# Two transformer blocks in one kernel: the first block's second half runs on 256 columns instead of 272, and its loops are written out

## The reference

```python
h = concatenate([meta, x], axis=1)                       # 16 + 256 tokens of 1024
u = rmsnorm(h, norm_mix_w); proj = u @ w_in
y_pool = pool_mixer(...)                                 # trailing windows of 2, 4, 8, 16 tokens
y_gla  = gla_mixer(...)                                  # gated linear attention, in chunks of 64
h = h + concatenate([y_pool, y_gla], -1) @ w_out         # token by token from here on
h = h + hier_moe(rmsnorm(h, norm_ffn_w), ...)            # 1 of 4 groups, 2 of its 4 experts
return rmsnorm(h, final_norm_w)[:, N_META:]              # the meta tokens' rows are dropped

def hier_moe(x, ...):
    combine = ...                                        # (tokens, 16) shares of the experts
    for e in range(16):
        y += combine[:, e] * ((silu(x @ w_gate[e]) * (x @ w_up[e])) @ w_down[e])
```

## Time and profile before

| | |
|---|---|
| Median of three runs | 2490.15 us |
| The profiled execution | 2492.44 us |
| Its span, first to last instruction | 2490.7 us |
| TensorE busy | 2289.7 us, 92% |
| VectorE busy | 1400.7 us, 56% |
| ScalarE busy | 779.3 us, 31% |
| GpSimd busy | 541.8 us, 22% |
| Mean granted TensorE clock | 0.953 |
| DMA over the span | 314.70 MB, 126 GB/s |

### The profile page before, as it was taken

How to read it: one execution, slowest core, us unless ns; L and a number is a source line. 1 busy time by engine, 2 the same in 40 slices (tenths; PEclk the granted TensorE clock), 3 DMA queues, 4 the chain that set the end, 5 groups by cost and what they waited for, 6 DMA issues and landing times.

```text
span 2490.7 us, 32942 instructions
## 1 busy us (share of the span) xinstructions
PE 2289.7 (92%) x12803; PEld 1938.0 (78%) x12803; DVE 1400.7 (56%) x1714; ACT 779.3 (31%) x1065; POOL 541.8 (22%) x298
## 2 busy tenths in 40 slices
PE   6686999979999998978989999989999997888997
PEld 5675999967888886855768888868888776658997
DVE  5635555766555547755477775555564225554444
ACT  3323444333222213244232222123222223344443
POOL 1001344003222002147132221013222001172430
PEclk9767999989999998989999999989999998999999
DMA  5302666853453454510245554444453334303663
GB/s 165 126 17 57 179 171 186 245 161 110 132 146 111 138 154 133 144 51 1 85 135 169 168 170 131 144 129 133 129 147 98 93 93 116 107 1 102 186 169 118
DMA packets 473572, 314.70 MB, mean 126 GB/s; under 512 B 26976, under 2 KB 435431, under 8 KB 473463
## 3 DMA queue, kind: packets, MB, share of 16 engines
q1 hardware_dynamic: 434294, 237.69, 34.2%
q10 hardware_dynamic: 39168, 75.51, 9.5%
HBM read 312.10 MB, written 1.05 MB: 126 GB/s over the span
## 4 chain that ended last, share of the span: by engine, by line
PE 78%; DVE 8%; ACT 5%; POOL 4%; issue 3%; DMA 1%; SPq 1%; POOLq 0%; DVEq 0%; ACTq 0%
PE ps L1394 23%; PE ps L1396 23%; PE ps L1395 23%; PE ps L1454 3%; POOL s L1376 2%; DVE ada_acc L866 2%; PE ps L1411 2%; ACT w_hi L555 2%; PE ps L1387 1%; POOL u_lo L1325 1%; DVE rstd L880 1%; DVE u_hi L894 1%; DVE st L1252 1%; ACT tmp_b L616 1%; PE ps L1741 1%
## 5 line engine op out<-in xcount | busy, mean ns | idle before, releaser
L1394 PE MATMUL ps<-u_hi,w_hi 128*128 128x512 f32 (+2 forms) x2528 | 883.0, 349 | 70.2 <-POOL u_lo L1325 59.8
L1395 PE MATMUL ps<-u_lo,w_hi 128*128 128x512 f32 (+2 forms) x2528 | 871.7, 345 | 0.0
L1396 PE MATMUL ps<-u_hi,w_lo 128*128 128x512 f32 (+2 forms) x2528 | 871.3, 345 | 0.0
L842 DVE TENSOR_TENSOR w_lo<-raw,w_hi 128x2048 fp32r<-128x2048 f32 (+1 forms) x238 | 504.7, 2121 | 235.4 <-ACT w_hi L555 234.5
L555 ACT CAST w_hi<-raw 128x2048 fp32r<-128x2048 f32 (+1 forms) x238 | 418.3, 1758 | 638.3 <-PE ps L1396 590.3
L1394 PEld LDWEIGHTS ps<-u_hi,w_hi 128*128 128x128 f32 x2528 | 485.2, 192 | 141.4 <-issue 65.4
L1396 PEld LDWEIGHTS ps<-u_hi,w_lo 128*128 128x128 f32 x2528 | 485.0, 192 | 54.2
L1395 PEld LDWEIGHTS ps<-u_lo,w_hi 128*128 128x128 f32 x2528 | 485.5, 192 | 52.1 <-issue 0.5
L866 DVE SCALAR_TENSOR_TENSOR ada_acc<-ada_w,sc_c,ada_acc 128x512 f32<-128x512 f32 x504 | 385.1, 826 | 4.4 <-DMA ada_w<-in_w_ada 4.4
L1332 POOL TENSOR_TENSOR hf_lo<-tmp_b,hf_hi 128x512 f32 (+3 forms) x88 | 230.9, 2624 | 644.2 <-ACT hf_hi L639 644.2
L635 ACT ACTIVATE tmp_a<-ps 128x512 f32<-128x512 f32 (+2 forms) x120 | 60.6, 505 | 729.4 <-PE ps L1396 650.3
(11 more groups left out here) (241 smaller groups left out, 1917.3 us busy)
## 6 DMA issues: line engine op xcount, KB each, us to landing
ada_w<-in_w_ada ACTq DMA_DIRECT2D x144, 512.0 KB, 3.6
raw<-in_w_ffn_gate SPq DMA_DIRECT2D x88, 512.0 KB, 4.0
raw<-in_w_ffn_up SPq DMA_DIRECT2D x88, 512.0 KB, 5.3
raw<-in_w_in SPq DMA_DIRECT2D x52, 512.0 KB, 4.7
raw<-in_w_ffn_down SPq DMA_DIRECT2D x64, 384.0 KB, 3.3
raw<-in_w_ffn_down SPq DMA_DIRECT2D x64, 320.0 KB, 3.8
raw<-in_w_expert_gate SPq DMA_DIRECT2D x32, 512.0 KB, 4.2
raw<-in_w_expert_up SPq DMA_DIRECT2D x32, 512.0 KB, 5.4
```

Source lines behind the costliest of these rows:

```text
L842: tt(w_lo[:, slot, 0:elems], raw[:, slot, 0:elems], w_hi[:, slot, 0:elems].bitcast(F32), ALU.subtract).then_inc(lo_done.sem, 1)
L1394: mm(acc, w1, m_hi, start=(first and i == 0), stop=False)
L1395: mm(acc, w1, m_lo, start=False, stop=False)
L1396: ins = mm(acc, w2, m_hi, start=False, stop=(last and i == n - 1))
```

## The change

Everything of the first block behind the mixer that ran on columns 0 to 271 runs on the 256 columns from 16 on: the output projection (its moving operand starts at column 16 of `u_hi` and `u_lo`), the residual's addition, the norm, the router, the experts. `h1` keeps its 272 columns, the new results go to columns 16 to 271. The router has two groups of 128 tokens instead of three. The mixers, which need the meta tokens, stay as they are.

`repeat` no longer makes a loop: all bodies of all ten stages, the second block's too, are written out on every engine.

```diff
 def repeat(eng, n, body):
-    if n <= 3:
-        for i in range(n):
-            body(i)
-        return
-    body(0)
-    with eng.Fori(1, n - 1) as i:
+    for i in range(n):
         body(i)
-    body(n - 1)
...
-        R2 = carve([("hm_hi", [P, MOE_F, T1], F32R), ("hm_lo", [P, MOE_F, T1], F32R), ("comb", [P, N_EXPERTS, T1], F32)])
+        R2 = carve([("hm_hi", [P, MOE_F, SEQ], F32R), ("hm_lo", [P, MOE_F, SEQ], F32R), ("comb", [P, N_EXPERTS, SEQ], F32)])
...
-            linear(st_out1, ("ffn1", h1, T1))
-            norm("ffn1", end_of(st_out1), h1, T1, scale=...,
-                 splits=((0, T1),), rows_squared=KD - 2)
+            linear(st_out1, ("ffn1", h1, SEQ, N_META))
+            norm("ffn1", end_of(st_out1), h1, SEQ, first=N_META, scale=...,
+                 splits=((0, SEQ),), rows_squared=KD - 2)
...
-                return tt(row(h1, m, 0, T1), acc[:, 0:T1], row(h1, m, 0, T1), ALU.add)
+                return tt(row(h1, m, N_META, T1), acc[:, 0:SEQ], row(h1, m, N_META, T1), ALU.add)
...
-                return tt(h1[:, 2 * i:2 * i + 2, :], acc[:, :, 0:T1], h1[:, 2 * i:2 * i + 2, :], ALU.add)
+                return tt(h1[:, 2 * i:2 * i + 2, N_META:T1], acc[:, :, 0:SEQ], h1[:, 2 * i:2 * i + 2, N_META:T1], ALU.add)
...
-            for t in range(3):
+            for t in range(2):
                 ins = tt(lg[:, t, :], ps[:, 7, 20 * t:20 * t + 20], rb[:, :], ALU.add)
...
-            nc.vector.tensor_copy(combT[:, 0:256], ps[0:16, 7, 0:256])
-            link(nc.vector.tensor_copy(combT[:, 256:272], ps[0:16, 7, 256 + 112:384]))
+            link(nc.vector.tensor_copy(combT[:, :], ps[0:16, 7, 0:SEQ]))
...
-            ffn_up(st_moe_a, moe_sig, T1, MOE_F, None, weighted=True)
+            ffn_up(st_moe_a, moe_sig, SEQ, MOE_F, None, weighted=True)
...
-            def rows_of(hi, lo, k0, n, T):
-                return [(hi[:, k, 0:T], lo[:, k, 0:T]) for k in range(k0, k0 + n)]
+            def rows_of(hi, lo, k0, n, T, c0=0):
+                return [(hi[:, k, c0:c0 + T], lo[:, k, c0:c0 + T]) for k in range(k0, k0 + n)]
...
-            linear(st_out1, T1, y_ready[0], squares="ffn1")
+            linear(st_out1, SEQ, y_ready[0], squares="ffn1", c0=N_META)
...
-            for t, c0 in enumerate((0, P, T1 - P)):
+            for t, c0 in enumerate((0, P)):
                 ins = turn(ps[:, 7, 20 * t:20 * t + 20], lgT[:, c0:c0 + P], 20)
...
-            ffn_up(st_moe_a, T1, MOE_F, None, None, behind_second=route)
-            ffn_down(st_moe_b, moe_sig, T1, 16, hm_hi, hm_lo, MOE_F, "moe_b", "end1", SEQ)
+            ffn_up(st_moe_a, SEQ, MOE_F, None, None, behind_second=route)
+            ffn_down(st_moe_b, moe_sig, SEQ, 16, hm_hi, hm_lo, MOE_F, "moe_b", "end1", SEQ)
```

More of the change, by code:

```diff
@@ L198, in program @@
         RG = carve([("g_pad", [P, 16, T1], F32), ("oT", [P, 4, T1], F32)])
-        R2 = carve([("hm_hi", [P, MOE_F, T1], F32R), ("hm_lo", [P, MOE_F, T1], F32R), ("comb", [P, N_EXPERTS, T1], F32)])
+        R2 = carve([("hm_hi", [P, MOE_F, SEQ], F32R), ("hm_lo", [P, MOE_F, SEQ], F32R), ("comb", [P, N_EXPERTS, SEQ], F32)])
         RR = carve([("wr", [P, KD, 20], F32), ("wr_hi", [P, KD, 20], F32R), ("wr_lo", [P, KD, 20], F32R),
[L201 to L205, removed]
+                    ("rb", [P, 20], F32), ("lg", [P, 2, 20], F32), ("r4a", [P, 2, 4], F32), ("r4b", [P, 2, 4], F32),
+                    ("r4c", [P, 2, 4], F32), ("oh_g", [P, 2, 4], F32), ("r1a", [P, 2], F32), ("r1b", [P, 2], F32),
+                    ("r1c", [P, 2], F32), ("pg", [P, 2], F32), ("r16", [P, 2, 16], F32), ("oh1", [P, 2, 4], F32),
+                    ("prob", [P, 2, 4], F32), ("combT", [16, SEQ], F32), ("lgT", [20, SEQ], F32),
+                    ("comb_hi", [16, SEQ], F32R), ("comb_lo", [16, SEQ], F32R), ("pick", [16, 16], F32R)])
         R3 = carve([("hf_hi", [P, FFN_F, T2], F32R), ("hf_lo", [P, FFN_F, T2], F32R)])
@@ L713, in _ @@
                 nc.scalar.copy(u_hi[:, 4 + h, 0:T1], oT[:, h, :]).then_inc(ev["gla_hi"], 1)
-            linear(st_out1, ("ffn1", h1, T1))
-            norm("ffn1", end_of(st_out1), h1, T1, scale=lambda k, q: vec[:, VEC["norm_ffn"][0] + k:VEC["norm_ffn"][0] + k + 1],
-                 splits=((0, T1),), rows_squared=KD - 2)
+            linear(st_out1, ("ffn1", h1, SEQ, N_META))
+            norm("ffn1", end_of(st_out1), h1, SEQ, first=N_META, scale=lambda k, q: vec[:, VEC["norm_ffn"][0] + k:VEC["norm_ffn"][0] + k + 1],
+                 splits=((0, SEQ),), rows_squared=KD - 2)
             act.wait_ge(ev["g_shift"], 1)
@@ L723, in _ @@
                 act.wait_ge(ev["share_sum"], e + 1)
-                nc.scalar.copy(comb[:, e, :], ps[:, 4 + e % 4, 0:T1]).then_inc(ev["share_out"], 1)
-            ffn_up(st_moe_a, moe_sig, T1, MOE_F, hm_hi, 0, None)
+                nc.scalar.copy(comb[:, e, :], ps[:, 4 + e % 4, 0:SEQ]).then_inc(ev["share_out"], 1)
+            ffn_up(st_moe_a, moe_sig, SEQ, MOE_F, hm_hi, 0, None)
             ffn_down(st_moe_b, 0, "moe_b", ("end1", h1, SEQ, N_META))
@@ L1104, in add_h1 @@
             def add_h1(i, acc):
-                return tt(h1[:, 2 * i:2 * i + 2, :], acc[:, :, 0:T1], h1[:, 2 * i:2 * i + 2, :], ALU.add)
+                return tt(h1[:, 2 * i:2 * i + 2, N_META:T1], acc[:, :, 0:SEQ], h1[:, 2 * i:2 * i + 2, N_META:T1], ALU.add)
             linear(st_out1, add_h1)
-            norm("ffn1", h1, T1)
+            norm("ffn1", h1, SEQ, first=N_META)
             dve.wait_ge(ld_router, 64)
@@ L1356, in _ @@
                    ALU.subtract).then_inc(y_ready[0].sem, 5 if h == 0 else 1)
-            norm("ffn1", T1)
-            ffn_up(moe_sig, T1, MOE_F, hm_hi, hm_lo)
+            norm("ffn1", SEQ)
+            ffn_up(moe_sig, SEQ, MOE_F, hm_hi, hm_lo)
             for l in range(2):
@@ L1427, in two_tiles, with linear @@
                         for t in range(2):
-                            ins = products(ps[:, 2 * g + t, 0:T], slot, [cols(t, k)], rows_of(u_hi, u_lo, k, 1, T), T,
+                            ins = products(ps[:, 2 * g + t, 0:T], slot, [cols(t, k)], rows_of(u_hi, u_lo, k, 1, T, c0), T,
                                            k == 0, k == KD - 1)
                 ins.then_inc(unit_done.sem, 1)
-            def linear(stg, T, ready=None, squares=None, ada=None, tail=None, behind=None, i0=0):
+            def linear(stg, T, ready=None, squares=None, ada=None, tail=None, behind=None, i0=0, c0=0):
                 for i in range(i0, stg["units"]):
@@ L1435, in linear @@
                     begin(u, g)
-                    two_tiles(u, g % 2, lambda t, k: 2 * P * k + P * t, T, ready if i == 0 else None)
+                    two_tiles(u, g % 2, lambda t, k: 2 * P * k + P * t, T, ready if i == 0 else None, c0)
                     if i == 0 and tail is not None:
@@ L1596, in _ @@
             pe.wait_ge(ev["o_root"], 4)
-            linear(st_out1, T1, y_ready[0], squares="ffn1")
-            norm("ffn1", T1, KD - 2)
+            linear(st_out1, SEQ, y_ready[0], squares="ffn1", c0=N_META)
+            norm("ffn1", SEQ, KD - 2)
             pe.wait_ge(ev["r_split"], 1)
```

20 lines of the change are left out of this document (10 added, 10 removed).

## The result

The changed kernel took 2472.99 us (median of four runs, 2470.36 to 2475.33), the kernel before 2490.91 beside it on the same chip: ratio 0.9927, 95% interval 0.9909 to 0.9944, so 17.9 us less (14 to 23). Two later series of the same kernel gave 0.9927 (0.9915 to 0.9939) and 0.9923 (0.9909 to 0.9937). The forecast was 15.0 us less, 2475.2, with a range of 2470 to 2482. The profiled execution took 2470.36 us with a span of 2468.6 at a clock of 0.955.

The account below looks back on a forecast made before the run. TensorE's matmul stream was taken to bound the expert stages and output projection. Gains of 15.5 us, 13.4 from full-clock columns, less give-back and fetches left 15.0 net: 2490.15 - 15.0 = 2475.2 us, range 2470 to 2482.

Parts of the forecast that it names:

- The bound and the trial in layer 1: Expert stages and output projection: matmuls alone set the time; step falls from 125.4 to layer 1's 120.0 ns, 13.4 us.
- its last paragraph: Signs to look for in the profile after, among them `st_moe_a`'s third to last unit 7.7 us shorter.
- The downs' columns: `st_moe_b`: 256 instead of 272 columns shorten the full-clock matmuls by 4.1 us.
- The output projection's columns and its offset: Output projection: columns gain 1.0 us; starting the operand at column 16 was taken to cost nothing, at most 1.0 us.
- Norm, router, shares: Chain between projection and experts: small gains, such as norm 0.3, router matmuls 0.3, spreading shares 0.3, fewer transposes and copies 0.4 us.
- The loops: Back edges on every engine: unrolling gains nothing, at most 28 x 0.21 = 5.9 us.
- The fetches: Instruction packets of straight code: 101 instead of 75; delayed weight loads cost 0.2 us in all, at most 31 us.
- Rival (c): Instruction fetches delay loads, each of 26 packets costing TensorE 1.2 us: 2506 us; chance 0.07, in whole or part.
- Rival (a): Downs held at old length by ada loads and VectorE's order: gain 10.9, 2479.3 us; chance 0.15, in whole or part.
- The end of the downs: End of `st_moe_b`: TensorE's wait for ada's last quarter grows, giving back 0.26 us.
- The sum: Whole kernel: 15.5 us gained, 15.2 after the downs' end, 15.0 net after fetches, giving 2475.2 us.
- the columns of the gates and ups: Gates and ups: 256 instead of 272 columns shorten the full-clock matmuls by 8.2 us, the largest term.

Follow-up runs that it names:

- e2: The changed kernel with the loops of before put back, 256 columns kept: 2473.39 us, ratio 0.9933 to the kernel before.
- e1: The kernel before with `repeat` written out and nothing else, 272 columns kept: 2490.87 us, ratio 1.0006 to the kernel before.
- e4: The changed kernel with ada's 16 loads beside the first block's downs bringing 32 of 512 columns each: 2470.02 us, ratio 0.9919.
- e5: The changed kernel with the output projection's moving operand starting at column 0 instead of 16: 2472.5 us in one run.
- e11: The changed kernel with the norm writing `u_hi` and `u_lo` at columns 16 to 271, read there by router, gates and ups: 2467.7 us, ratio 0.9913.
- e13: The changed kernel with the norm writing at columns 128 to 383, read there by router, gates and ups: 2474.0 us in one run.
- e8: The changed kernel with the downs' four ada chunks spread over the gates and ups, sums one unit behind the last multiply-adds: 2484.9 us, ratio 0.9976.
- e10: The changed kernel with the downs' ada chunks under the gates and ups, sums two units behind the last multiply-adds: 2468.3 us, ratio 0.9914.
- e7: The changed kernel with TensorE's products in both expert stages on 192 columns, 64 tokens' results left out: 2459.51 us in one run.

## Why the prediction held, step by step

- **The bound and the trial in layer 1.** Right: the gates and ups run at 120.0 ns, and e2 shows that the columns alone carry the time. 7.3 us of the forecast 7.8 came (7.7 in its last paragraph, without the half-clock steps); in the third unit 18 steps run at half clock where 12 did before.
- **The downs' columns.** The term was 4.1 us, from a step of 120.0. In the changed kernel it is 118.4 (79 steps from 454.95 to 464.30), against 125.2 in the kernel before, and e2's downs, nearly without gaps, gained 4.9. The term was too small by 0.8. The experts' buffers also got a new row length, 1024 bytes for 1088; that this is the cause was not tried.
- **The output projection's columns and its offset.** "I take nothing" for the offset was wrong in its sign: it pays 2.2 ns a step or more, 0.4 us in the changed kernel's trace, and is part of the 1.6 measured.
- **Norm, router, shares.** 2.8 us where 2.2 stood; each term was small and right in kind.
- **The loops.** Nothing in the whole time, as forecast (e1). The bound of 5.9 us was not needed. One place does differ, the end of the downs, below.
- **The fetches.** 101 packets, exactly. "0.2 us in all" was too small: at least one packet of the 26 falls on a place where a load comes just in time, and costs about a microsecond. Rival (c) had the mechanism right and the count wrong.
- **Rival (a)** came in part: of the 4.9 us that the narrower downs can give, 0.8 to 1.6 went back, through VectorE's order, as its row said, but set off by the packet and not by the bytes (e4).
- **The end of the downs.** Here the step failed that should have cost 0.3 us: the wait ahead of ada's sums was to grow from 4.35 to 4.6 us and shrank to 3.1. The last quarter's load took 4.5 us, not 7.48 as in the earlier trace rows. That isn't the columns' doing. From the last matmul of the downs to the sums it takes 4.69 us in the kernel before and 4.62 in e2, both with loops, and 3.4 to 3.7 in the seven written-out traces with 256 or 272 columns and all of ada (the changed kernel's three, e1, e5, e11, e13); the last load takes 7.5 and 7.1 us in the first two and 4.5 to 6.1 in the seven. So the written-out code gains 1.2 us here; what in it does so is open. The rows of e2 and e1:

```profile
515.36 0.28 PE L1395 MATMUL ps<-hm_hi,w_lo 128*128 128x256 f32 x1
...
519.98 3.57 PE L1453 MATMUL ps<-base,ada_acc 128*128 128x1 f32 x16 [3.91 <-DVE ada_acc L866]
```

```profile
532.23 0.29 PE L1390 MATMUL ps<-hm_hi,w_lo 128*128 128x272 f32 x1
...
535.69 3.20 PE L1448 MATMUL ps<-base,ada_acc 128*128 128x1 f32 x16 [2.75 <-DVE ada_acc L860]
```

- **Luck.** The sums behind that wait ran in 1.95 us where the kernel before took 3.57. That moves with the clock and not with the change: the three traces of the changed kernel have 1.95, 3.57 and 1.95. So up to 1.6 of the 2.4 us in the table's last row is luck of that one execution.
- **The sum.** 15.0 was forecast and 17.6 to 20.4 measured. In the first block it is 17.4 for 14.9: projection, norm and shares bring 0.9 more, the end 2.7 more, the gates and ups 0.5 less and the downs 0.6 less, their shorter step against their gaps. That the time came within 3 us is thus partly errors that cancel; the main term, the columns of the gates and ups, is what held. In the second block nothing came or went in the feed-forwards: ScalarE's high part of unit 64 starts 17.75 us earlier than before, and so does that of unit 96. By the last unit it is 22.4 us, but the 4.6 come at norms and in attention, where e1 too differs from the kernel before, by 1.8 us at the last unit.

## What to carry to other kernels

A stage that runs the new shape already, elsewhere in the same kernel, prices a change better than any formula; but look at row length and start of the operand too, since the same 256 columns stepped at 113, 118 and 120 ns. Fewer columns soon stop paying: 64 fewer brought the step from 120.0 only to 111.7 ns, and probably the weight loads pace it there. When work moves to another stage, count in which unit its producer really ends: one unit too early turned a gain of about 4 us into a loss of 12, part of it by the clock that fell behind each wait and its sums.

## What the runs showed of the hardware that was not expected

- The matmul step depends on where the moving operand lies: 120.0 ns from column 0 or 128 of a 2048-byte row, 113.3 to 118.0 from column 16, all at 256 columns and full clock; 118.4 in rows of 1024 bytes (the downs).
- At 192 columns the step is 111.7 ns, and with one column 106.
- One 16 KB packet for instructions made the downs' loads beside it 1.1 to 1.7 us slower (4.4 to between 5.5 and 6.1) in every written-out trace compared; in looped e2, where it falls 6 us earlier, the loads there took 5.8. The gates' loads beside a packet were not slower (4.2 us with and without).
- A wait of TensorE of 1.97 us and 1.95 us of one-column sums behind it, in a stream at full clock, were followed by a granted clock of 0.90 and then 0.67, mixtures of its two levels, in the next two stretches of 4 us (e8). Such sums without the wait (e10) and a wait of 1.94 us without sums (e7) left it at 1.00; with 192 columns (e7) it once fell behind sums without a wait.
